# Second expert stretch: GpSimd makes the low parts of all later table rows, the vector engine makes none of them

## The reference, cut to what matters

```
def peer(x, wq, keys, u_tab, v_tab):              # x: T x 1024, u_tab and v_tab: 16384 x 1024
    q = (xb @ wq).reshape(PEER_BLOCK, PEER_HEADS, 2, PEER_HALF)
    s = einsum('thpd,hpnd->thpn', q, keys)
    sv, si = top_k(s, 16)                         # per token, head and half
    cv, ci = top_k(all sums of the two halves, 16)
    e = i1 * 128 + i2                             # 8 heads x 16 experts per token
    gate = softmax(cv)
    act = gelu(einsum('td,thkd->thk', xb, u_tab[e]))
    return einsum('thk,thkd->td', gate * act, v_tab[e])
```

## Time and profile before

| what | value |
|---|---|
| median of 3 runs | 4843.45 us (4841.42 to 4846.25) |
| the profiled execution | 4840.01 us, its span 4838.2 us |
| busy in the span | PE 4334.9, DVE 2828.5, POOL 2135.2, ACT 1521.8 us |
| granted TensorE clock, mean | 0.926 |
| second stretch of layer 0 (1120 to 1790 us) | 670 us: PE 562.48, DVE 422.05, POOL 455.27, ACT 190.30 us busy |
| second stretch of layer 1 (3530 to 4194 us) | 664 us: PE 563.17, DVE 418.66, POOL 450.36, ACT 187.17 us busy |

### The profile page before, as it was taken

How to read it: one execution, slowest core, us unless ns; L and a number is a source line. 1 busy time by engine, 2 the same in 40 slices (tenths; PEclk the granted TensorE clock), 3 DMA queues, 4 the chain that set the end, 5 groups by cost and what they waited for, 6 DMA issues and landing times.

```text
span 4838.2 us, 58142 instructions
## 1 busy us (share of the span) xinstructions
PE 4334.9 (90%) x22794; PEld 3593.9 (74%) x22794; DVE 2828.5 (58%) x4699; ACT 1521.8 (31%) x2235; POOL 2135.2 (44%) x1326
## 2 busy tenths in 40 slices
PE   8797889999888889999997888799988888899998
PEld 4566669998777778888455576699977777788883
DVE  5445318963676665777264543289446676657762
ACT  1213125543222233333112131255422222333331
POOL 0232028897777644111003230388876776541110
PEclk9877899999999999999997678999999999999999
DMA  3102125665776787998021021266656767889970
GB/s 102 22 18 10 40 74 189 212 226 183 243 260 228 257 289 257 333 319 289 3 76 22 10 10 40 76 220 219 214 195 227 263 234 253 297 268 327 326 247 20
DMA packets 389776, 858.56 MB, mean 177 GB/s; under 512 B 88320, under 2 KB 236032, under 8 KB 385792
## 3 DMA queue, kind: packets, MB, share of 16 engines
q1 hardware_dynamic: 266624, 577.76, 36.8%
q0 software_dynamic: 67584, 201.57, 12.2%
q10 hardware_dynamic: 55296, 75.52, 4.2%
HBM read 723.16 MB, written 131.54 MB: 177 GB/s over the span
## 4 chain that ended last, share of the span: by engine, by line
PE 61%; DVE 21%; POOL 6%; DMA 5%; ACT 4%; issue 3%; SPq 0%; ACTq 0%; DVEq 0%; POOLq 0%
PE banks L1257 22%; PE banks L1192 8%; PE banks L757 7%; DMA peer_gates<-peer_v,u_stage 4%; PE banks L1122 3%; PE banks L1285 3%; PE banks L1237 2%; PE banks L1204 2%; PE banks L1143 2%; POOL u_stage L1793 2%; PE banks L845 2%; DVE normed L2393 2%; DVE x L2373 2%; DVE x L2370 1%; DVE peer_scores L2276 1%
## 5 line engine op out<-in xcount | busy, mean ns | idle before, releaser
L1257 PE MATMUL banks<-v_parts,gated_parts 128*128 128x512 f32 x4608 | 1048.2, 390 | 8.1 <-DVE gated_parts L2434 8.1
L1257 PEld LDWEIGHTS banks<-v_parts,gated_parts 128*128 128x128 f32 x4608 | 867.1, 188 | 189.1 <-issue 8.8
L1785 POOL DMA_INDIRECT peer_gates<-peer_v,u_stage x384 | 503.3, 1311 | 972.9 <-DVE normed L2430 590.8
L1192 PE MATMUL banks<-peer_x_parts,u_parts 128*128 128x448 f32 x3168 | 683.7, 374 | 8.8 <-DVE u_parts L2379 8.8
L1192 PEld LDWEIGHTS banks<-peer_x_parts,u_parts 128*128 128x128 f32 x3168 | 603.4, 193 | 59.7 <-DVE u_parts L2379 9.5
L2415 DVE TENSOR_TENSOR v_parts<-v_stage,v_parts 128x1024 fp32r<-128x1024 f32 x256 | 313.6, 1225 | 309.6 <-ACT v_parts L1665 309.5
L2393 DVE SCALAR_TENSOR_TENSOR normed<-peer_gates,u_stage,normed 128x1024 f32<-128x1024 f32 x254 | 384.3, 1513 | 167.2 <-DMA peer_gates<-peer_v,u_stage 152.2
L1665 ACT ACTIVATE v_parts<-v_stage 128x1024 fp32r<-128x1024 f32 x256 | 271.4, 1060 | 634.2 <-PE banks L1257 628.9
L1237 PE MATMUL banks<-x 128*128 128x128 f32 x1536 | 242.8, 323 | 195.6 <-DVE x L2373 195.6
L1192 PE MATMUL banks<-peer_x_parts,low_s 128*128 128x448 f32 x1696 | 405.9, 372 | 0.0
L1237 PEld LDWEIGHTS banks<-x 128*128 128x128 f32 x1536 | 224.7, 232 | 226.8 <-DVE x L2373 216.7
(11 more groups left out here) (336 smaller groups left out, 7526.0 us busy)
## 6 DMA issues: line engine op xcount, KB each, us to landing
v_stage<-peer_v SPq DMA_DIRECT2D x256, 512.0 KB, 5.0
u_stage<-peer_ut SPq DMA_DIRECT2D x244, 512.0 KB, 4.8
dense_gelus<-u_stage ACTq DMA_DIRECT2D x256, 224.0 KB, 4.9
gates<-peer_gates SPq DMA_DIRECT2D x16, 3072.0 KB, 10.7
u_stage<-gates SPq DMA_DIRECT2D x64, 768.0 KB, 7.1
gated<-dense_gelus SPq DMA_DIRECT2D x256, 192.0 KB, 5.7
x<-peer_ut SPq DMA_DIRECT2D x64, 512.0 KB, 4.8
u_raw<-peer_ut SPq DMA_DIRECT2D x64, 512.0 KB, 5.2
```

The costliest lines, as they stand in the source:

```text
L1192: ins = mm(PS[:, d % 2, 0:DW], u_part(n, a, k), XR[:, b, k, DENSE0:TOK], start=(k == 0 and m == 0), stop=(k == KT - 1 and m == 2))
L1257: ins = mm(vo[2 * t + half], HR[:, s, a, t * 128:(t + 1) * 128], VR[:, s, b, half * 512:(half + 1) * 512], start=(j == 0 and m == 0), stop ...
L1785: eng.indirect_dma_start(out=GU[:, t % 4, :], out_offset=None, in_=din["peer_v"].rearrange("l i j d -> (l i j) d"), in_offset=bass.Indirec ...
```

## The change

All 88 low parts of a layer's second stretch are made on GpSimd. The vector engine's function `low_u`, its call ahead of the loop and its calls in the loop are gone, and with them the semaphore `u_low_dve`. On GpSimd the low parts of rows 0 and 1 are now both made ahead of the loop, and the loop has the low part of every row q+2. What a dense row and a raw load wait for (`low_ready`) is now one counter. `LOADS` is 128 + 88. Nothing is computed differently. Line numbers behind the removed lines are 5 to 20 lower in the kernel after.

```diff
-    u_hi, u_low, u_low_dve = sem("u_hi"), sem("u_low"), sem("u_low_dve")
+    u_hi, u_low = sem("u_hi"), sem("u_low")
...
     def low_ready(L, n):
 
-        if n < NKEYS:
-            return u_low, (NKEYS + NL // 2) * L + n + 1
-        q = n - NKEYS
-        if q % 2:
-            return u_low_dve, NL // 2 * L + q // 2 + 1
-        return u_low, (NKEYS + NL // 2) * L + NKEYS + q // 2 + 1
+        return u_low, LOADS * L + n + 1
...
-            for n in range(NKEYS + 1):
+            for n in range(NKEYS + 2):
                 low_u(n)
...
             for g in range(STEPS):
                 for q in rows_of_step(g):
-                    if q + 2 < NL and q % 2 == 0:
+                    if q + 2 < NL:
                         low_u(NKEYS + q + 2)
...
-            def low_u(q):
-
-                dve.wait_ge(u_hi, LOADS * L + NKEYS + q + 1)
-                raw, high, low = u_place(NKEYS + q)
-                TT(low, raw, high.bitcast(F32), ALU.subtract).then_inc(u_low_dve, 1)
-
...
             one_hots(0)
-            low_u(1)
             for g in range(STEPS):
-                for q in rows_of_step(g):
-                    if q + 2 < NL and q % 2:
-                        low_u(q + 2)
                 if g + 1 < UNITS:
                     one_hots(g + 1)
```

## The result

Measured in the same session, the kernel after takes 4853.73 us (median of 20 runs, 4841.27 to 4866.95) and the kernel before 4845.34 us (20 runs, 4838.38 to 4850.38). The ratio is 1.002, with a 95% interval of 1.0011 to 1.0028. The medians are 8.4 us apart, 0.17%, which is under the 0.2% that the prediction took as its bound for "no change". The interval leaves out 1, so between these runs the change is a small loss, and its upper end lies over that bound. The forecast was 4845 us in a range of 4790 to 4892.

A forecast was written before the change was run, and what follows sets the result against it. TensorE was bound by late triplets: low parts mid block, transfers behind gate stores. Per layer 14.5 - 5.8 - 2.4 - 5.6 = +0.7 us, two layers +1.4 on 4840.0, median 3.4 higher: 4845 us, range 4790 to 4892.

The forecast's parts named there:

- room case: Middle blocks: GpSimd has enough room, period near 72 us, 4784 us in all; chance 0.24, for all periods under 76.0.
- ring case: Behind gate stores, GpSimd's waits stay beside its new low parts: period 81.3 us, 4895 us in all; chance 0.20.
- The head: Layer's start to step E of block one: GpSimd arrives 14.5 us later, its gathers starting 9.5 us late.
- the end: From slot 104, column gathers over: TensorE is the bound again and waits go, -2.4 and -5.6 us a layer.
- the middle: Six blocks between step E of blocks one and seven: 77.1 us each instead of 78.06, 5.8 us less.
- GpSimd becomes the bound: Repeating blocks: GpSimd needs 77.1 us, TensorE 65.6; period between 76.0 and 78.2, 4831 to 4858 us, chance 0.44.
- The period P: Time GpSimd needs for one block's queue when hardly ever waiting: 77.1 us, bounds 72 and 81.3 us.
- I keep 0.8 us: Behind a gate store: of GpSimd's 3.4 us of waits for its ring, 0.8 us a block stay.
- The excess of the transfers: Lengthening of GpSimd's indirect transfers by the vector engine: 71.1 to 63.3 us, a gain of 1.6 us a block.
- The four waits of C to F: Last block, scatters of steps C to F: waits of 1.39 us on average go, -5.6 us a layer.
- The term of -2.4 us for A and B: Last block, behind the store: two low parts of 1.217 us ahead of triplets A and B go, -2.4 us.
- GpSimd pays for the meetings: GpSimd's low part waits for any scalar_tensor_tensor it meets, 1.7 us a block: period 78.8 us, 4867 us; chance 0.12.

The follow-up runs named there:

- e4: Kernel before, with the vector engine's low part made behind the triplet instead of ahead of it: ratio 0.9715 to the kernel before, -141 us.
- e8: Kernel before with only every fourth column gather issued: ratio 0.9918 to the kernel before.
- e10: Kernel before with the low part behind the triplet and each gate store cut into four pieces: ratio 0.9640 to the kernel before.
- e7: The whole change with only every fourth column gather issued: ratio 0.9760 to the kernel before.
- e9: The whole change with each gate store cut into four pieces, spread over the next block's raw loads: ratio 0.9989 to the kernel before.
- e5: The whole change run again, on another chip: ratio 1.0009 to the kernel before.
- e1_head: Kernel before, with GpSimd taking over only the low parts of later rows 1, 3, 5 and 7: ratio 1.0047 to the kernel before, some +23 us.
- e6: The whole change, but the low part of row 3 behind the first eight column gathers: ratio 1.0006 to the kernel before.
- e3_end: Kernel before, with GpSimd taking over only the low parts of odd rows 73 to 87: ratio 0.9975 to the kernel before, -12 us.
- e12: Kernel before with the low part behind the triplet, only every fourth low part on GpSimd, gate store in four pieces: ratio 0.9552 to the kernel before.
- e11: Kernel before with the low part behind the triplet and only every fourth low part on GpSimd: ratio 0.9680 to the kernel before.

## Why the prediction came out right, point by point

**How much the hit says.** The range of 4790 to 4892 us spans 2% and reaches from near the room case to near the ring case, so that the time lies in it says little. The median is 8.7 us above the named time. In the traces the two stretches came out 15.6 us longer, where 1.4 was forecast. The head and the end agree with the sum on average; the middle, forecast at -5.8 us a layer, was +5.7 and -4.1. What speaks for the prediction is the mechanism, point by point below.

**What bounded the kernel before: right.** The prediction had the triplets late, for the low parts of the change and for transfers behind a store. e4 and e8 show the first, e10 the second.

**GpSimd becomes the bound: right, and shown; one sign of it was wrong.** Its busy share is 86 and 88% (predicted: over 85%), its waits for the vector engine are all but gone, and e7 against e8 and e9 tell a bound GpSimd from one that rests. The waits of C, D and E at the scatter went, as forecast. But TensorE was to wait at dense rows "instead of at the scatter", and most of its waiting is still at the scatter, of A and B behind a store and of F. The runs don't part in full how much of that is the burst of the store and how much late issue by GpSimd; with the burst spread (e9), 34.4 of the 60.3 us stay. The prediction listed "TensorE still waits for triplets in B to E" as a sign of being wrong; of these only B does, twice in five blocks of layer 0, once for 7.4 us.

**The period P: mechanism right, size low by 1 us.** Predicted 77.1; in the session of the result it was 79.0 and 77.3, on average 78.2, and on the slower chip of e5 78.6 and 79.2. The forecast's own bracket was 76.0 to 78.2, and the prediction had itself set P over 77.8 as "slower". By its formula such a P gives some 4857 us; 4853.7 was measured. Two terms of the sum were small. Without waits the sum was 77.1 - 0.8 = 76.3 us, and GpSimd's bare queue is 77.1 to 77.6 (e9, and layer 1 of after): a low part takes 2.54 us on average in layer 0 (126.9 / 50), not 2.43, and all ten of a block pay that. "I keep 0.8 us" for waits that stay was 2.2 us a block in layer 0 of after (10.8 us in five), 6.8 of the 10.8 for ScalarE's high part, which the sum didn't have at all; in layer 1 no such wait shows. The excess of the transfers, which I had scaled, held: 215.7 - 161 x 0.94 = 64.4 us, predicted 63.3.

**The head: right in total.** Predicted +14.5 us a layer, measured +15.6 and +14.2 by the same marks. e1_head alone cost 23 us for two layers (13 to 33), 11.6 a layer. The rows of the timeline of after at the head:

```profile
1132.41 3.10 POOL L1773 TENSOR_TENSOR u_parts<-u_stage,u_parts 128x1024 fp32r<-128x1024 f32 x1 [2.47 <-DVE x L2368]
1143.64 2.40 POOL L1773 TENSOR_TENSOR low_s<-normed,low_s 128x1024 fp32r<-128x1024 f32 x1 [8.14 <-ACT low_s L1578]
1146.21 1.13 POOL L1788 DMA_INDIRECT u_stage<-gelus,u_stage  x1 [0.16 <-issue]
...
1207.84 2.41 POOL L1773 TENSOR_TENSOR u_parts<-u_stage,u_parts 128x1024 fp32r<-128x1024 f32 x1
```

The first gather starts 19.7 us behind the first triplet, in the earlier trace rows 7.0 us behind it: 12.7 us later, 3.2 more than the 9.5 of the sum, since the high part of row 3 itself came 3.0 us later (17.1 us behind the first triplet against 14.2). From the first gather to step E it is 61.6 us against 58.7, +2.9, where the sum had 5.0: a column gather there took 1.09 us on average instead of 1.20. Two errors of opposite sign, so that the total is better than its terms is luck. e6 shows that GpSimd's rest in front of row 3 can't simply be filled: in layer 0 its first gather came 9.2 us earlier than in e5, the first gate store only 4.0.

**The end: total right, one term wrong.** Predicted -8.0, measured -7.4 and -8.4 us by the same marks; e3_end gives -12 us for both layers, -6 each. The scatters of D and E in the last block of after (timeline) have no wait; before, each of C to F had one:

```profile
1732.76 1.95 PE L1232 MATMUL banks<-x 128*128 128x128 f32 x16
1744.26 1.95 PE L1232 MATMUL banks<-x 128*128 128x128 f32 x16
```

The four waits of C to F are gone, as forecast: from C's scatter to the last store it takes 5.1 us less in both layers (predicted -5.6). The term of -2.4 us for A and B failed. Their waits behind the store were 3.28 and 2.49 us before and are 3.85 and 4.44 after in layer 0, 3.19 and 3.04 against 2.95 and 5.39 in layer 1: some 2 us more instead of 2.4 less. So the last block, which was to be 8 us shorter, is only 3.6 and 2.3 us shorter between its stores. Another 3.3 and 4.2 us of the -7.4 and -8.4 are the moved mark at step E of block seven, and the rest, 0.5 and 1.8 us, lies behind the last store. That the total agrees is luck.

**The rivals.** *Room* (P near 72) is out: no stretch of five blocks of the change has a mean under 77 us. *The ring behind the store* (P = 81.3) is what happens in single blocks of 83 us, not in the mean: its place and its chain were right. e9, which takes it away, shows its mean price: a block takes 77.2 us on average over the five of both layers, 78.4 in after, so 1.1 us a block. *GpSimd pays for the meetings* (P = 78.8, a low part 0.17 us longer; by the formula 4865 us, not the 4867 that the prediction gives): it is 0.11 us longer, so this rival is partly true. The trace has meetings of both kinds (below), and the vector engine pays for most of them. By the rule of the Trainium skill's page "SBUF — State Buffer", section "SBUF: two separate sides", GpSimd would have paid for all in which it came second; by the starts that the profile records, the trace has that only for some.

**What the prediction didn't see.** It asked whether GpSimd's 14.3 us of waits were room or the ring's. They were room, and the change used it up: 12.2 us of low parts, with the gaps and the shorter transfers, went in, and what stays of the waits is 0.8 us a block or less. What it didn't see is where they came from: e4 takes them from 71.7 to 17.1 us by an edit on the vector engine alone, and is worth 2.9%. It also took TensorE's 65.6 us as fixed, which e12 refutes.

## What to carry to other kernels

Before work is moved off an engine because another waits for it, look at where it stands in that engine's queue: the low part was late because it stood ahead of the triplet, and moving it behind the triplet was worth 2.9%, handing it to another engine nothing. Before idle time is taken for room, add up the queue with the gaps between instructions: here 14.3 us of waits a block took in 12 us of new work, and the receiving engine became the bound. Count as well at what moment its queue starts: the delay at the head was not made up, neither in the change nor in e1_head, where GpSimd still rested in every block. When two waits of different origin overlap (here the triplet's and the burst behind the store), mend the one that holds the pace first: the spread store was worth 0.2 to 0.3% beside the change, 0.75% behind the reordering, and 1.3% where GpSimd had the most room (e11 to e12). These are differences of ratios from different chips and sessions, with intervals of 0.1 to 0.3% each way, so their order is safer than their sizes.

## What the runs showed of the hardware

**A GpSimd subtraction stops the vector engine, mostly for its whole length.** Two meetings in the timeline of the change run again, each a slot and a low part:

```profile
1279.83 3.70 DVE L2382 SCALAR_TENSOR_TENSOR normed<-peer_gates,u_stage,normed 128x1024 f32<-128x1024 f32 x1 [1.88 <-DMA peer_gates<-peer_v,u_stage]
1280.04 2.40 POOL L1773 TENSOR_TENSOR u_parts<-u_stage,u_parts 128x1024 fp32r<-128x1024 f32 x1
...
1476.84 1.28 DVE L2382 SCALAR_TENSOR_TENSOR normed<-peer_gates,u_stage,normed 128x1024 f32<-128x1024 f32 x1 [1.36 <-DMA peer_gates<-peer_v,u_stage]
1477.57 2.76 POOL L1773 TENSOR_TENSOR u_parts<-u_stage,u_parts 128x1024 fp32r<-128x1024 f32 x1
```

In the first the slot had begun 0.21 us earlier and still took 1.28 + 2.4 us. In the second it had run for 0.73 us, finished in its usual 1.28, and the low part took 0.36 us more. So in the first the vector engine paid for the whole low part; in the second GpSimd paid 0.36 us, about what the slot had left (0.55). In after, from 1285 to 1406 us, six single vector instructions had a low part start 0.72 to 0.93 us behind them, and all kept their 1.22 or 1.28 us; in the earlier trace rows it started 0.65 us behind, and the slot paid. A span on GpSimd is rough: if its starts are recorded some 0.7 us late, the engine that really came first wins each time, and no run here decides that. Size is no shelter: a 128 x 16 operation of the vector engine, 0.17 us otherwise, took 3.35 us beside two low parts of the change. This is why the vector engine is busy for longer with fewer instructions: its slots cost 564.6 us over the kernel, before 384.3.

**The same matmuls cost less when TensorE doesn't wait.** The matmuls of five blocks took 327.75 us at a granted clock of 0.93, and 303.95 at 0.98 in e12, 24 of the 77 us that five blocks got shorter. Most of it is the scatters, the matmuls right behind the waits: 78.5 us before, 62.2 in e12. A scatter of 16 matmuls takes 1.95 us without a wait and 3.78 behind a wait of 4.67 us or of 15.24 us in the change. The granted clock is 1.00 during the scatter at 1732.76 of after and 0.50 during both slow ones, that is 2.4 GHz against 1.2. So a wait can cost more than its length, and the busy time of a kernel with waits is no floor.
